# Splitting two slab loads of each looped expert by partitions, in a two-layer trunk with a mixture of experts

## Chip, cores and metric

One NeuronCore of one Trainium2 chip runs the whole kernel. The metric is the device time of one execution in microseconds (us); lower is better. The inputs lie in HBM before the start, and the output has to be in HBM at the end.

## What is computed

256 tokens of width 1024 pass two layers. Each layer has a mixer (three kinds of attention side by side) and a feed-forward part. The feed-forward part of layer 0 is dense; that of layer 1 is a mixture of eight experts, of which each token uses two. The change touches only the loads of the experts' weights.

```python
def swiglu(h, w_gate_up, w_down):
    gt, up = jnp.split(h @ w_gate_up, 2, axis=-1)
    return (jax.nn.silu(gt) * up) @ w_down

def moe_swiglu(h, w_router, w_gate_up, w_down):
    ...
    top_val, top_idx = lax.top_k(logits, TOP_K)
    top_w = jax.nn.softmax(top_val, axis=-1)
    ...
    for e in range(N_EXPERTS):
        y = y + combine[:, e:e + 1] * swiglu(t, w_gate_up[e], w_down[e])
    return y.reshape(b_, s_len, dm)
```

All of it is float32. One expert has 1024 x 7168 weights for gate and up and 3584 x 1024 for down: 42 MB in all (11.0 million numbers of four bytes).

## The kernel before

The first part (mixers, dense feed-forward part, router) ends near 735 us of the span. Its weights come in slabs of 512 KB and are of no concern here.

**Slabs of an expert.** The weights of each expert are laid out in HBM as 42 slabs (`EXP_SLABS`) of 1 MB, each 128 partitions x 2048 floats, so a partition's row of a slab is 8 KB. They are stored three by three: for each partition, the rows of three slabs (`LOAD = 3`) lie behind one another. SBUF holds a ring of 21 slabs (`exp_raw`, `EXP_RAW = 21`); slab j of any expert goes to place j % 21.

**Order of the loads.** All loads are issued by the SP engine, in the order in which TensorE reads the slabs. The first expert and the second one are loaded slab by slab (`first_slabs`, `single_slabs`, lines 583 to 607). From the third expert on a loop of the machine runs, `sp.Fori(2, slots)` at line 650, whose body is `expert_slabs` (line 609): slabs 0 to 38 in 13 loads of three slabs (3 MB, line 612), then slabs 39, 40 and 41 (`END = 39`) each as a load of its own (1 MB, line 618). Before each load SP waits on `slab_used`, a count that TensorE raises by one after the last matmul on a slab (lines 2348 and 2382); a load waits until its place in the ring is free. With these inputs eight slots are computed, one for each expert, so the loop body runs six times.

**Order of the reading.** On TensorE, `expert` (line 2328) goes through the slabs: 8 of gate and up, 8 of gate and up, 4 of down, 8 of gate and up, 4 of down, 4 of gate and up, and 6 of down. The last pieces are `down(STEPS - 2, ...)` on slabs 36 and 37, the turning of the next tokens and of the hidden values, and `down` on slabs 38, 39, 40 and 41 (lines 2412 to 2418). `wait_slab` (line 369) makes TensorE wait before a slab: on `first_ready` in the first two experts, then once per load of three on `more_ready`, and on `end_ready` for slabs 39 to 41. A load raises its semaphore by 16 when it has landed. Experts with up to 64 tokens are computed in two blocks of 32 tokens, larger ones in three (`BLOCKS_AT = (3, 2, 3, 2, 3, 3, 2)`, and two for the eighth), and TensorE needs half as long again for a slab in three blocks.

The semaphores of a loop's iteration i are waited for against a multiple of i. The first two experts don't use `more_ready` and `end_ready`, so SP raises these once by what two iterations would have given (lines 642 to 644).

```python
elif j >= END:
    pe.wait_ge(end_ready[j - END], i * 16 + 16)
...
for j in range(END, EXP_SLABS):
    sp.wait_ge(slab_used, i * EXP_SLABS + (PRE + j + 1 - EXP_RAW))
    sp.dma_start(exp_slots[j % EXP_RAW], moe_slabs[bass.ds(e, 1), j // LOAD, :, j % LOAD, :]
                 .rearrange("e p n -> (e p) n"))\
        .then_inc(end_ready[j - END], 16)
```

Of the kernel before, what the change touches and what calls it, by code (L numbers as in the profile page):

```python
# [13 lines left out]
P = 128  # L14
# [26 lines left out]
EXP_RAW, LOAD = 21, 3  # L41
SINGLE_SLOTS = 2
# [12 lines left out]
EXP_SLABS = sum(GU) + sum(DN)  # L55
# [110 lines left out]
def trunk(nc, x_in, mem_in, mix_norm_g, w_in, sb_q_g, sb_k_g, gla_a_up, gla_a_b, gla_o_g, ca_q_g,  # L166
# [10 lines left out]
    with ExitStack() as ctx:  # L177
        def sb(name, shape, dt=F32):
            return ctx.enter_context(nc.sbuf_tensor(name, shape, dt))

        def sem(name):
            return ctx.enter_context(nc.semaphore(name))
# [51 lines left out]
        exp_raw = sb("exp_raw", [P, EXP_RAW, EXP_SLAB])  # L234
# [12 lines left out]
        exp_slots = [exp_raw[:, n, :] for n in range(EXP_RAW)]  # L247
# [111 lines left out]
        end_ready = [sem(f"end_ready{i}") for i in range(LOAD)]  # L359

        END = EXP_SLABS - LOAD

        def load_ready(i, j):

            if j % EXP_RAW == END % EXP_RAW:
                return i * 16
            return i * (16 * EXP_SLABS // EXP_RAW) + 16 * (j // EXP_RAW)

        def wait_slab(pe, i, j):

            if type(i) is int and i * EXP_SLABS + j < SINGLE:
                pe.wait_ge(first_ready[j % EXP_RAW], 16 * ((i * EXP_SLABS + j) // EXP_RAW + 1))
            elif j >= END:
                pe.wait_ge(end_ready[j - END], i * 16 + 16)
            elif j % LOAD == 0:
                pe.wait_ge(more_ready[j % EXP_RAW // LOAD], load_ready(i, j))

# [32 lines left out]
        def raw_slot(j):  # L410
            return w_raw[:, j % RAW, :]
# [152 lines left out]
        @block.sync  # L564
        def _(sp):
            sp.dma_start(hn[:, 0, :], memory_in[:, 0, :]).then_inc(first_tile[0], 16)
            sp.dma_start(gain[:, :], mem_norm_g[0].rearrange("(o d) -> o d", o=1)
                         .broadcast_to([P, DM])).then_inc(first_gain, 16)
            sp.dma_start(hn[:, 1, :], memory_in[:, 1, :]).then_inc(first_tile[1], 16)
            EARLY = {20: 1, 16: 1, 15: 1, 13: 1, 12: 1, 10: 1, 4: 1, 3: 1, 2: 1, 1: 2}  # L570

            branch1 = [p for p in table if p.name == "branch1"][-1]
            last_gate = [p for p in table if p.name == "gate1"][-1]

            def first_slabs():
                for j in (0, 1, 2, 3, 4, 20, 5, 6, 7, 17, 18, 9, 10, 11, 12, 13, 14, 15, 8, 16, 19):
                    if j == 0:
                        sp.wait_ge(branch_lo, BRANCHES + 1)
                    elif j == 1:
                        sp.wait_ge(branch_lo, BRANCHES + 2)  # L580
                    elif j == 4:
                        sp.wait_ge(ca_max, LAYERS)
                    elif j == 20:
                        sp.wait_ge(slab_used, branch1.end)
                    elif j == 5:
                        sp.wait_ge(branch_lo, BRANCHES + 3)
                    elif j == 17:
                        sp.wait_ge(slab_used, last_gate.end)
                    elif j == 9:
                        sp.wait_ge(lo_ready, PRE)  # L590
                    elif j == 11:
                        sp.wait_ge(slab_used, PRE)
                    elif j == 8:
                        sp.wait_ge(norm_done, NT * 3 * LAYERS)
                    elif j == 19:
                        sp.wait_ge(route_logit, NT)
                    sp.dma_start(exp_slots[j], moe_slabs[0, j // LOAD, :, j % LOAD, :])\
                        .then_inc(first_ready[j], 16)
                    yield

            def single_slabs(e, i, js):
                for j in js:
# [3 lines that stand above are left out]
                        .then_inc(first_ready[j % EXP_RAW], 16)  # L606

            def expert_slabs(e, i, begin=0):
                for j in range(begin, END, LOAD):
                    sp.wait_ge(slab_used, i * EXP_SLABS + (PRE + j + LOAD - EXP_RAW))  # L610
                    n = j % EXP_RAW
                    sp.dma_start(exp_raw[:, n:n + LOAD, :].rearrange("p a n -> p (a n)"),
                                 moe_slabs[bass.ds(e, 1), j // LOAD]
                                 .rearrange("e p a n -> (e p) (a n)"))\
                        .then_inc(more_ready[n // LOAD], 16)
                for j in range(END, EXP_SLABS):
                    sp.wait_ge(slab_used, i * EXP_SLABS + (PRE + j + 1 - EXP_RAW))
                    sp.dma_start(exp_slots[j % EXP_RAW], moe_slabs[bass.ds(e, 1), j // LOAD, :, j % LOAD, :]
                                 .rearrange("e p n -> (e p) n"))\
                        .then_inc(end_ready[j - END], 16)  # L620

            first = first_slabs()
            for s, src in enumerate(flat):
                if s == 2:
                    sp.dma_start(xs[:, :, :], tokens).then_inc(x_loaded, 16)
                if s == 8 * RAW:
                    sp.dma_start(route_w[:, :, :], moe_router[0].rearrange("(k p) n -> p k n", p=P))\
                        .then_inc(route_loaded, 16)
                if s >= RAW:
                    sp.wait_ge(lo_ready, s - RAW + 1)  # L630
                dst = raw_slot(s)[:, 0:sizes[s]]
                if len(src.shape) == 3:
                    dst = dst.rearrange("p (k n) -> p k n", k=src.shape[1])
                sp.dma_start(dst, src).then_inc(raw_ready[s % RAW], 16)

                for _ in range(EARLY.get(PRE - s, 0)):
                    next(first)

            for _ in first:
                pass  # L640
            for n in range(EXP_RAW // LOAD):
                sp.sem_inc(more_ready[n], load_ready(SINGLE_SLOTS, n * LOAD) - 16)
            for n in range(LOAD):
                sp.sem_inc(end_ready[n], SINGLE_SLOTS * 16)
            single_slabs(0, 0, range(EXP_RAW, EXP_SLABS))
            sp.wait_ge(r_table, 1)
            slots = sp.value_load(slot_i[0:1, 0:1], min_val=EXPERTS, max_val=SLOTS)
            e = sp.value_load(slot_i[0:1, 2:3], min_val=0, max_val=EXPERTS - 1)
            single_slabs(e, 1, range(EXP_SLABS))
            with sp.Fori(2, slots) as i:  # L650
                e = sp.value_load(slot_i[0:1, bass.ds(i + 1, 1)], min_val=0, max_val=EXPERTS - 1)
                expert_slabs(e, i)
            for t in range(NT):
                sp.wait_ge(added, slots * NT + (t + 1))
                sp.dma_start(result[:, t, :], xs[:, t, :]).then_inc(stored, 16)
            sp.wait_ge(stored, NT * 16)
# [1192 lines left out]
        def _(pe):  # L1849
# [478 lines left out]
            def expert(i, blocks, blocks_ago):  # L2328
                j = 0

                def gate_and_up(s, part):
                    nonlocal j
                    w = 2 * lanes_wide(s)
                    n = KT // GU[s]
                    for q in part:
                        wait_slab(pe, i, j)
                        for kk in range(n):
                            k = q * n + kk
                            if is_first(i) and (s, k) == (0, KT // 2):
                                pe.wait_ge(x_dve, 1)  # L2340
                            for b in range(blocks):
                                for g in range(LANES):
                                    c = kk * LANES * w + g * w
                                    ins = mm(lane(pa, g)[:, b * BW:b * BW + w],
                                             xf[:, k, b * LANE:(b + 1) * LANE],
                                             exp_slots[j % EXP_RAW][:, c:c + w],
                                             k == 0, k == KT - 1)
                        ins.then_inc(slab_used, 1)
                        j += 1
# [142 lines left out]
```

## Time and profile before

| | |
|---|---|
| median of 3 runs | 1571.69 us (1571.23 to 1571.84) |
| the profiled execution's own time | 1571.44 us |
| its span, first to last instruction | 1569.6 us |
| mean granted clock of TensorE | 0.991 |
| TensorE busy with matmuls | 1534.0 us (98%) |
| VectorE, ScalarE, GpSimd busy | 521.6, 457.0, 90.3 us |
| moved by DMA | 485.63 MB, 309 GB/s on average |

The span is that of the profiled execution, and all times of the trace count from its start. PE is TensorE's matmuls, PEld its weight loads, DVE is VectorE, ACT ScalarE, POOL GpSimd, SP the engine that issues the loads. A matmul's end is modelled, so a busy TensorE isn't necessarily at its peak. The DMA share is the mean over the core's 16 DMA engines: 1.00 is all of them busy.

### The profile page before, as it was taken

The page shows a single profiled execution, that of the slowest core. Times are in us where ns is not written, and L with a number is a line of the kernel's source. Part 1 is how long each engine was busy: PE and PEld are TensorE (multiplying, and loading weights), DVE is VectorE, ACT ScalarE, POOL GpSimd, SP SyncE. Part 2 cuts the span into 40 slices and gives each one's busy share as a digit, 9 for nine tenths or more (in the row PEclk, how much of TensorE's full clock was granted, in tenths as well). Part 3 has the DMA queues.
Part 4 walks back from the last instruction along what each step waited for, and adds up shares of the span by engine and source line. Part 5 has one row for each costly group of instructions (what it writes and reads, how often), then busy time and mean ns, then how long its engine had stood idle before and what let it go on. Part 6 is the DMA issues. An engine that isn't in the chain of part 4 may idle for free.

```text
span 1569.6 us, 31360 instructions
## 1 busy us (share of the span) xinstructions
PE 1534.0 (98%) x14130; PEld 967.9 (62%) x14130; DVE 521.6 (33%) x619; ACT 457.0 (29%) x598; POOL 90.3 (6%) x128
## 2 busy tenths in 40 slices
PE   7999999999999999999999999999999999999877
PEld 6888888788888888888345453454534534544324
DVE  5755575655567565665200101001000000010001
ACT  5557653544455567452000000000000000000000
POOL 5211100000002110001000000000000000000000
PEclk9999999999999999999999999999999999999989
DMA  7555455666656554777999999999999999999995
GB/s 272 178 158 161 148 174 161 210 193 188 188 174 188 163 175 145 242 279 287 420 418 392 411 427 427 423 431 424 425 429 429 425 426 427 422 417 427 428 426 238
DMA packets 87778, 485.63 MB, mean 309 GB/s; under 512 B 10528, under 2 KB 12640, under 8 KB 64608
## 3 DMA queue, kind: packets, MB, share of 16 engines
q1 hardware_dynamic: 84592, 474.67, 78.6%
q0 software_dynamic: 3056, 8.99, 1.6%
q8 instruction: 111, 1.82, 0.5%
q14 instruction: 19, 0.16, 0.0%
HBM read 481.53 MB, written 2.10 MB: 308 GB/s over the span
## 4 chain that ended last, share of the span: by engine, by line
PE 86%; DMA 9%; DVE 2%; POOL 2%; issue 1%; ACT 0%; SPq 0%; DVEq 0%; POOLq 0%; ACTq 0%
PE pa L2075 28%; PE ps L2075 18%; PE pa L1946 12%; PE pa L1948 12%; PE pa L1947 12%; DMA exp_raw<-in_moe_slabs 8%; PE ps L2354 1%; DVE w_lo L1268 1%; DMA w_raw<-in_w_mem_kv 1%; POOL hrs L763 1%; POOL head_gains L692 0%; PE ps L2324 0%; PE ps L1873 0%; PE ps L2248 0%; PE ps L2069 0%
## 5 line engine op out<-in xcount | busy, mean ns | idle before, releaser
L2075 PE MATMUL pa<-exp_raw,xf 128*32 128x512 f32 (+1 forms) x5120 | 501.0, 544 | 14.5 <-DMA exp_raw<-in_moe_slabs 13.7
L2075 PEld LDWEIGHTS pa<-exp_raw,xf 128*32 128x32 f32 x5120 | 163.3, 110 | 308.8 <-issue 261.2
L1268 DVE TENSOR_TENSOR w_lo<-w_raw,w_hi 128x1024 fp32r<-128x1024 f32 x226 | 274.2, 1232 | 122.2 <-ACT w_hi L898 113.2
L898 ACT ACTIVATE w_hi<-w_raw 128x1024 fp32r<-128x1024 f32 (+1 forms) x228 | 236.9, 1053 | 148.9 <-PE pa L1948 146.9
L2075 PE MATMUL ps<-exp_raw,hf 128*32 128x256 f32 x4480 | 251.5, 383 | 5.5 <-DMA exp_raw<-in_moe_slabs 5.5
L1946 PE MATMUL pa<-w_hi,r 128*128 128x512 f32 x600 | 240.3, 400 | 1.9 <-DVE r L1303 1.8
L1947 PE MATMUL pa<-w_lo,r 128*128 128x512 f32 x600 | 234.6, 391 | 0.0
L1948 PE MATMUL pa<-w_hi,r 128*128 128x512 f32 x600 | 234.5, 391 | 0.0
L2075 PEld LDWEIGHTS ps<-exp_raw,hf 128*32 128x32 f32 x4480 | 146.4, 111 | 111.7 <-issue 17.6
L1821 DVE TENSOR_TENSOR hs<-pa,hs 128x768 f32<-128x768 f32 (+3 forms) x32 | 23.7, 742 | 464.9 <-ACT hs L1224 464.9
L1946 PEld LDWEIGHTS pa<-w_hi,r 128*128 128x128 f32 x600 | 113.0, 188 | 29.4 <-issue 3.2
L1948 PEld LDWEIGHTS pa<-w_hi,r 128*128 128x128 f32 x600 | 113.0, 188 | 24.2
L1947 PEld LDWEIGHTS pa<-w_lo,r 128*128 128x128 f32 x600 | 113.2, 189 | 22.0
L1946 PE MATMUL pa<-w_hi,xt 128*128 128x512 f32 (+1 forms) x320 | 123.2, 385 | 3.0 <-DVE xt L1303 2.7
L1948 PE MATMUL pa<-w_hi,xt 128*128 128x512 f32 (+1 forms) x320 | 121.3, 379 | 0.0
L1947 PE MATMUL pa<-w_lo,xt 128*128 128x512 f32 (+1 forms) x320 | 121.2, 379 | 0.0
L1224 ACT ACTIVATE hs<-pa 128x768 f32<-128x768 f32 (+3 forms) x32 | 20.4, 637 | 314.7 <-PE pa L2075 314.7
L1214 ACT ACTIVATE hf<-ps 128x512 f32<-128x512 f32 x24 | 14.3, 597 | 290.5 <-PE ps L2354 290.5
L1946 PEld LDWEIGHTS pa<-w_hi,xt 128*128 128x128 f32 x320 | 60.2, 188 | 16.1 <-issue 2.7
L1948 PEld LDWEIGHTS pa<-w_hi,xt 128*128 128x128 f32 x320 | 60.2, 188 | 11.3
L1947 PEld LDWEIGHTS pa<-w_lo,xt 128*128 128x128 f32 x320 | 60.3, 188 | 10.6
L1808 DVE COPY hf<-ps 128x256 f32<-128x256 f32 x12 | 5.1, 424 | 163.4 <-PE ps L2354 163.4
(274 smaller groups left out, 859.3 us busy)
## 6 DMA issues: line engine op xcount, KB each, us to landing
exp_raw<-in_moe_slabs SPq DMA_DIRECT2D x78, 3072.0 KB, 31.3
exp_raw<-in_moe_slabs SPq DMA_DIRECT2D x102, 1024.0 KB, 10.2
w_raw<-in_w_in SPq DMA_DIRECT2D x104, 512.0 KB, 4.4
w_raw<-in_ff_w_gate_up SPq DMA_DIRECT2D x44, 512.0 KB, 4.5
w_raw<-in_ff_w_down SPq DMA_DIRECT2D x22, 512.0 KB, 4.1
w_raw<-in_w_mem_kv SPq DMA_DIRECT2D x16, 512.0 KB, 5.5
w_raw<-in_w_out SPq DMA_DIRECT2D x16, 512.0 KB, 4.3
w_raw<-in_w_br_sb SPq DMA_DIRECT2D x8, 512.0 KB, 3.6
```

The costliest lines, as they stand in the source:

```text
L763: pool.tensor_tensor(dst[:, 0:n], src[:, 0:n], half[:, 0:n], ALU.pow)\
L898: act.activation(dst, raw, ACT.Copy).then_inc(hi_ready, 1)
L1214: act.activation(hf[:, s % 2, 0:m, :], turned_hidden(s)[:, 0:m, :], ACT.Copy)\
L1224: act.activation(hidden_rows(s, blocks), gate_up(s, 0, blocks), ACT.Silu)\
L1268: dve.tensor_tensor(dst, raw, hi.bitcast(F32), ALU.subtract)\
L1808: dve.tensor_copy(hf[:, s % 2, 4:2 * blocks, :], turned_hidden(s)[:, 4:2 * blocks, :]).then_inc(e_dve, 1)
L1821: dve.tensor_tensor(hidden_rows(s, blocks), gate_up(s, 1, blocks), hidden_rows(s, blocks), ALU.mult).then_inc(e_h, 1)
L1946: pe.matmul(dst, hi, m_hi, start=first, stop=False)
L1947: pe.matmul(dst, hi, m_lo, start=False, stop=False)
L1948: return pe.matmul(dst, lo, m_hi, start=False, stop=last)
L2075: return pe.matmul(dst, a, b, start=start, stop=stop, skip_group_check=True)
L2354: ins = pe.transpose(turned_hidden(s)[:, m, :], hs[:, m * P:(m + 1) * P], ident[:, :])
```

## The change

Each of slabs 39 and 40 of a looped expert is loaded by three DMAs in place of one: partitions 0 to 111, partitions 112 to 119, and partitions 120 to 127, all with 8 KB per partition as before. Slab 41, the loads of three slabs, and the first two experts stay as they are. By its description the load of 112 partitions is done by all 16 DMA engines (seven rows each) and each load of eight partitions by the low eight of them (one row each). Every part raises the slab's `end_ready` semaphore by 16, so the multiple that TensorE waits for is 48 in place of 16 for slabs 39 and 40, and SP's one-time raise is three times as large for these.

```diff
         END = EXP_SLABS - LOAD
+        LOW_DMAS = P // 16
+        PARTS = [(0, P - 2 * LOW_DMAS), (P - 2 * LOW_DMAS, P - LOW_DMAS), (P - LOW_DMAS, P)]
+
+        def end_parts(j):
+
+            return PARTS if j < EXP_SLABS - 1 else [(0, P)]
...
             elif j >= END:
-                pe.wait_ge(end_ready[j - END], i * 16 + 16)
+                n = 16 * len(end_parts(j))
+                pe.wait_ge(end_ready[j - END], i * n + n)
...
                 for j in range(END, EXP_SLABS):
                     sp.wait_ge(slab_used, i * EXP_SLABS + (PRE + j + 1 - EXP_RAW))
-                    sp.dma_start(exp_slots[j % EXP_RAW], moe_slabs[bass.ds(e, 1), j // LOAD, :, j % LOAD, :]
-                                 .rearrange("e p n -> (e p) n"))\
-                        .then_inc(end_ready[j - END], 16)
+                    for a, b in end_parts(j):
+                        sp.dma_start(exp_raw[a:b, j % EXP_RAW, :],
+                                     moe_slabs[bass.ds(e, 1), j // LOAD, a:b, j % LOAD, :]
+                                     .rearrange("e p n -> (e p) n"))\
+                            .then_inc(end_ready[j - END], 16)
...
             for n in range(LOAD):
-                sp.sem_inc(end_ready[n], SINGLE_SLOTS * 16)
+                sp.sem_inc(end_ready[n], SINGLE_SLOTS * 16 * len(end_parts(END + n)))
```

On the other engines the order of the instructions is the same. On SP, these are the rows at the end of the loop's body before (the last load of three slabs, then slabs 39, 40 and 41; `exp_raw` is the ring, `in_moe_slabs` the weights in HBM):

```order
L612 DMA exp_raw<-in_moe_slabs 128x6144
L617 REGISTER_ALU
L618 ISA [waits slab_used]
L618 DMA exp_raw<-in_moe_slabs 128x2048
L617 REGISTER_ALU
L618 ISA [waits slab_used]
L618 DMA exp_raw<-in_moe_slabs 128x2048
L617 REGISTER_ALU
L618 ISA [waits slab_used]
L618 DMA exp_raw<-in_moe_slabs 128x2048
L650 REGISTER_ALU
```

And these stand there on SP now, from slab 40 to the loop's end (slab 39 is as slab 40):

```order
L624 REGISTER_ALU
L626 ISA [waits slab_used]
L626 DMA exp_raw<-in_moe_slabs 112x2048
L626 ISA
L626 DMA exp_raw<-in_moe_slabs 8x2048
L626 ISA
L626 DMA exp_raw<-in_moe_slabs 8x2048
L624 REGISTER_ALU
L626 ISA [waits slab_used]
L626 DMA exp_raw<-in_moe_slabs 128x2048
L659 REGISTER_ALU
```

One wait still stands ahead of each slab. Two DMAs of eight partitions follow that of 112 without a wait, and slab 41's load stands behind them: four DMAs more in each pass of the loop.

## Rows read from the trace of the kernel before

**Rows 1.** The page: busy tenths, granted clock and DMA in 40 slices of the span.

```profile
PE   7999999999999999999999999999999999999877
PEclk9999999999999999999999999999999999999989
DMA  7555455666656554777999999999999999999995
GB/s 272 178 158 161 148 174 161 210 193 188 188 174 188 163 175 145 242 279 287 420 418 392 411 427 427 423 431 424 425 429 429 425 426 427 422 417 427 428 426 238
```

**Rows 2.** Waits of PE, 745 to 1450 us: who, for whom, us, times, longest.

```profile
PE pa L2075 <- DMA exp_raw<-in_moe_slabs: 2.8, 1, 2.8
PE pa L2075 <- DVE hs L1821: 0.8, 1, 0.8
PE ps L2075 <- DMA exp_raw<-in_moe_slabs: 0.4, 1, 0.4
```

**Rows 3.** The same view, 1450 to 1562 us.

```profile
PE pa L2075 <- DMA exp_raw<-in_moe_slabs: 10.9, 8, 2.0
PE ps L2075 <- DMA exp_raw<-in_moe_slabs: 5.1, 3, 3.6
```

**Rows 4.** Chain that ended last, from 1440 us: start us, us, what.

```profile
1453.14 43.30 DMA exp_raw<-in_moe_slabs
...
1502.06 47.69 DMA exp_raw<-in_moe_slabs
1549.75 0.14 issue
1549.88 3.66 PE ps L2075 x64
1553.55 1.02 PE ps L2324 x8
1554.57 0.22 PE pa L2354 x2
1554.79 7.09 PE ps L2075 x128
```

**Rows 5.** Timeline of PE, last expert: start, us, instructions, [idle before <- releaser].

```profile
1520.54 5.36 PE L2075 MATMUL pa<-exp_raw,xf 128*32 128x512 f32 x48 [1.17 <-DMA exp_raw<-in_moe_slabs]
1527.84 3.28 PE L2075 MATMUL pa<-exp_raw,xf 128*32 128x512 f32 x16 [1.95 <-DMA exp_raw<-in_moe_slabs]
...
1535.17 3.66 PE L2075 MATMUL ps<-exp_raw,hf 128*32 128x256 f32 x64 [0.26 <-DMA exp_raw<-in_moe_slabs]
...
1542.50 1.93 PE L2075 MATMUL pa<-exp_raw,xf 128*32 128x256 f32 x32 [1.94 <-DMA exp_raw<-in_moe_slabs]
...
1549.88 3.66 PE L2075 MATMUL ps<-exp_raw,hf 128*32 128x256 f32 x64 [1.27 <-DMA exp_raw<-in_moe_slabs]
```

**Rows 6.** Windows: stretch, length, busy by engine, clock, DMA share, GB/s.

```profile
1540.00:1544.00 4.00, 2.06 (x40) 1.02 (x36) 0.00 (x0) 0.00 (x0) 0.00 (x0) 1.00 1.02 426
1545.00:1547.00 2.00, 2.00 (x41) 1.23 (x44) 0.00 (x0) 0.60 (x1) 0.00 (x0) 1.00 0.51 217
1547.00:1550.00 3.00, 1.73 (x36) 0.85 (x32) 0.42 (x1) 0.38 (x1) 0.00 (x0) 1.00 0.46 191
1550.00:1553.00 3.00, 3.00 (x60) 2.18 (x61) 0.00 (x0) 0.00 (x0) 0.00 (x0) 1.00 0.51 213
1553.00:1556.00 3.00, 3.00 (x46) 1.94 (x42) 0.42 (x1) 0.66 (x2) 0.00 (x0) 1.00 0.43 169
1556.00:1558.00 2.00, 2.00 (x45) 1.19 (x39) 0.00 (x0) 0.00 (x0) 0.00 (x0) 1.00 0.07 25
```

**Rows 7.** DMA by queue, 745 to 1558 us: packets, MB, share of 16 engines.

```profile
q1 hardware_dynamic: 23422, 334.10, 97.4%
q0 software_dynamic: 1315, 4.80, 1.5%
q8 instruction: 82, 1.34, 0.7%
q14 instruction: 5, 0.04, 0.0%
```

**Rows 8.** Source view of L612, loads of three slabs: ns min/median/max; us to landing.

```profile
L612 SPq DMA_DIRECT2D exp_raw<-in_moe_slabs x78: 332/333/337, 907.0 to 1502.1; - x78
...
DMA to landing us min/median/max: 19.7/31.3/48.4
```

**Rows 9.** Source view of L618, slabs 39 to 41: ns min/median/max; us to landing.

```profile
L618 SPq FUSED_REGOPS  x18: 37/37/37, 994.8 to 1513.7; - x18
L618 SPq MOVE exp_raw<-in_moe_slabs x18: 29/29/29, 994.9 to 1513.8; - x18
L618 SPq DMA_DIRECT2D exp_raw<-in_moe_slabs x18: 332/333/333, 994.9 to 1513.8; - x18
...
DMA to landing us min/median/max: 25.3/32.9/43.4
```

## The prediction, made before the changed kernel ran

> **What bounds the kernel now.** I read the page's slices first. From slice 20 on (about 745 us) the DMA row stands at 9 and the rate at 392 to 431 GB/s, up to the last slice [rows 1]. TensorE stands at 9 there as well, so two resources look full, and the waits have to tell which one sets the end. From 745 to 1450 us TensorE waits 3.2 us in all for slabs [rows 2], from 1450 us on 16.0 us, in eleven waits (8 + 3) [rows 3]. TensorE is behind while experts come in three blocks, and catches up in the last ones. The chain that ended last says the same: two long pieces of DMA lead to 1549.75 us, then TensorE works without a stop to about 1561.9 us [rows 4]. The wait that ends at 1549.88 us is for the load that holds slabs 36 to 38 of the last expert. So the end is that landing plus a fixed tail of matmuls, scatter and store, and the landing is the end of an unbroken stream of transfers. **A microsecond off the stream ahead of that landing is a microsecond off the end**, until the 16.0 us of waits are used up.
>
> Is the stream ever dry? A load of three slabs never lands in less than 19.7 us after its issue, and the single slabs take 25.3 us or more [rows 8, 9]. The waits of the last expert end at 1520.54, 1527.84, 1535.17, 1542.50 and 1549.88 us, about 7.33 us apart [rows 5], so three slabs need 7.33 us. At least 12 us of work is always queued. SP's issuing sets nothing.
>
> Now the look that matters for this change: are the 16 DMA engines equally late? The windows over the end say no. The DMA share is 1.02 up to 1544 us, then 0.51, 0.46, 0.51 and 0.43 from 1545 to 1556 us, then 0.07 [rows 6]. **Half of the engines finish their part of the stream near 1545 us, the other half near 1556 us, some 10.5 us later**, and TensorE waits for the late half each time. Each engine has the same rows of weights to move, so the late ones do something else besides. The queues show it: 82 instruction packets of 16 KB (1.34 MB), 0.7% of 16 engines' time in 813 us, which is 0.007 x 16 x 813 = 91 us of engine time, about 1.1 us each [rows 7]. Spread over eight engines that is 11.4 us each, close to the 10.5 us; over all 16 there would be no two halves. I take it that TensorE's instructions are fetched by eight of the engines.
>
> **The change, part by part.** *Rows moved.* A slab is eight rows of 8 KB for each engine. Slabs 39 and 40 become seven rows for each engine and two more for the low eight: nine for these, seven for the high eight. A row costs 7.33 / 24 = 0.305 us (24 rows of a load of three, on the late half) [rows 5]. The landing that sets the end is that of slabs 36 to 38 of the sixth pass; ahead of it lie five passes with two split slabs each, ten slabs. If the late half is the high half, its stream is ten rows shorter: 10 x 0.305 = **3.05 us earlier**. The early half gets 3.05 us more and still finishes 10.5 - 6.1 = 4.4 us ahead. Slabs 39 and 40 of the sixth pass are moved behind the deciding wait: the stream ends before 1558 us with slab 41 [rows 6], so slab 40 is there a slab's time earlier, before 1556 us; slabs 38 to 41 are read in turn in 7.09 us from 1554.79 us on [rows 4], slab 40 from 1558.3 us. They are in time and stay so. Worth 0 there.
>
> *More DMAs on SP.* Four more in each pass, each 37 + 29 + 333 ns [rows 9]: 1.6 us. Ahead of every landing lie at least 12 us of queued work [rows 5, 8], so this is hidden: 0. If that cover were gone, it would be 1.6 us per pass, 8 us by the deciding wait.
>
> *More completion marks.* Three where there was one. The trace doesn't show what one costs an engine; single slabs and loads of three have one mark for 8 and for 24 rows. As a bound, the whole difference between the share of the loads, 97.4%, and full use, less instructions and the small queue, is 100 - 97.4 - 1.5 - 0.7 = 0.4% of 813 us, 3.3 us for the marks of all 159 loads, 0.02 us each [rows 7]. The low engines get two more in each of ten slabs, the high ones none: at most 0.4 us, on the early half. 0 on the path.
>
> *Where the rows land.* In a load of 128 partitions every engine writes partitions that are its own. A load of eight partitions has eight engines writing at once to eight neighbouring partitions, and the 112 are dealt out in other portions. No transfer of this size on fewer than 128 partitions is in the trace, so nothing prices it. The lower bound is no cost, since it's the same number of rows of 8 KB; a gain over 0.305 us a row has no reason, as the engines are full. The upper bound is that the engines of such a load are served in turn. I take no cost, the nearest row being the ordinary row time, and keep the turns for a rival. The break-even: the low half has 4.4 us in hand after the move, so its split slab may cost 0.44 us more than nine plain rows before it becomes the late half, and 10.5 - 3.05 = 7.45 us, so 0.75 us a slab, before the kernel is slower than now.
>
> **Sum** against the profiled execution: 1571.44 - 3.05 = 1568.39 us. Its own time is 0.25 us under the median of the runs, 1571.69 us; against that, 1571.69 - 3.05 = **1568.6 us**. A measurement of this kernel can tell about 0.2% from no change, which is 3.14 us. So my forecast lies on that edge, and I split its chance evenly.
>
> **Rivals.**
>
> *Served in turn (slower).* Suppose four of the eight engines of a small load share one way into SBUF. Then its row takes 4 x 0.305 = 1.22 us in place of 0.305, twice per slab: 1.83 us more. The low half loses 10 x (0.305 + 1.83) = 21.4 us by the deciding landing, has 10.5 us in hand, and ends 10.9 us later than the late half does now: 1571.69 + 10.9 = **1582.6 us**. If the high engines, whose rows go to the same partitions, are held up too (half of the 1.22 us a slab), another 6 us: 1588. For it: the rate of 425 GB/s over so long [rows 1] says that whatever is full has no room to catch up. Against it: writes could be buffered, and the early half can spare 7.45 us. It decides from 0.75 us a slab. The Trainium skill speaks for this rival (SBUF — State Buffer, section Door 1: the DMA port swizzle): the 128 partitions hang on 16 ports, four neighbours to a port, so partitions 112 to 119 reach only two ports, and its measured table gives four partitions 27.6 GB/s against 328 for all. Eight rows of 8 KB through two such ports would take, as an estimate from that page, 1.2 us, and the time would be this rival's. No run here shows it yet.
>
> *Partly eaten.* A smaller cost of the same kind, 0.45 to 0.75 us a slab: the low half becomes the late one and the gain shrinks from 3.05 to 0 us. 1568.7 to **1571.7**.
>
> *The late half is not the high half.* No view names a DMA engine, so the trace can't say which eight fetch instructions. If they are the low ones (or some of them are), the change loads the late engines with ten rows more: 1571.69 + 3.05 = **1574.7 us**. Nothing in the rows speaks for or against; it could as well be half, and 0.12 is a judgement.
>
> *It doesn't do what it says.* If the loads of eight partitions were dealt to all or to high engines, the late half would gain less than ten rows or lose some; that lies between 1568.6 and 1574.7, in the cases above.
>
> **How the numbers follow.** The forecast, 1568.6 (own range 1567.8 to 1569.3), has 0.50. A gain a little above the edge for reasons I don't see: 0.02, faster. Partly eaten: 0.10, no change. Low half is the late one: 0.12, at +3.05 us just under the edge, so half no change and half slower. Served in turn: 0.26, slower. Faster by over 0.2%: 0.25 + 0.02 = 0.27. Within: 0.25 + 0.10 + 0.06 = 0.41. Slower: 0.06 + 0.26 = 0.32. For eight times in ten the range takes in all but the last rival (0.74) and the near quarter of that one: from 1567.3 to 1580.0 us.
>
> **What would show it.** Right: the stretch of half DMA share before the end shrinks from 10.5 to about 4.4 us less a slab's share; the wait that ended at 1549.88 us ends near 1546.8; TensorE's waits from 1450 us on sum to about 13.0 us in place of 16.0. Served in turn: DMA share stays near 1 while GB/s falls in the stretch where slabs 39 and 40 are served, once per pass, and the half-share stretch at the end is gone or turned round. Low half late: the half-share stretch grows from 10.5 to some 16.6 us, with the last wait near 1553. Wrong altogether: the last wait at 1549.9 with an unchanged stretch, or waits of TensorE for slab 39 or 40 in the middle passes.

## The result, and the profile after

Each kernel ran four times. The changed one took 1649.89 us (median; 1646.38 to 1653.89), the one before 1571.76 us (1571.23 to 1572.61). The ratio is 1.0494 (95% interval 1.0482 to 1.0507): **slower by 78.1 us, 13.0 us for each of the six passes of the loop**. The forecast was 1568.6 us, and the range ended at 1580.0 us. The profiled execution of the changed kernel took 1646.38 us by its own time, 74.9 us more than that of the kernel before.

The page of the changed kernel, busy tenths and DMA in 40 slices of its span (41.1 us each):

```profile
PE   8999999999999999999999999996899999976776
PEclk9999999999999999999999999999999999998998
DMA  7555444766565555779999999999999999999994
GB/s 270 176 161 165 142 154 157 242 186 194 160 203 179 164 154 186 277 287 417 414 386 415 427 426 364 385 427 319 425 427 295 429 425 265 428 427 273 429 405 144
```

The row to read is the last one, against [rows 1]. The DMA row stays at 9 as before, but the rate, which held 392 to 431 GB/s from slice 20 on, now falls to 364 and 385, 319, 295, 265 and 273 GB/s, once in each of the first five passes. The engines are as busy as ever and move less. The windows over two of these places show how deep the holes are (columns as in [rows 6]; the DMA share and the rate stand last):

```profile
1000.00:1010.00 10.00, 10.00 (x98) 3.31 (x94) 0.39 (x1) 0.39 (x1) 0.00 (x0) 1.00 1.00 427
1010.00:1020.00 10.00, 10.00 (x100) 3.08 (x96) 0.03 (x1) 0.20 (x1) 0.00 (x0) 1.00 1.02 348
1020.00:1030.00 10.00, 10.00 (x192) 6.25 (x186) 0.96 (x1) 0.81 (x1) 0.00 (x0) 1.00 1.00 194
1030.00:1040.00 10.00, 8.41 (x144) 6.37 (x140) 0.42 (x1) 0.60 (x1) 0.00 (x0) 1.00 1.04 314
1040.00:1050.00 10.00, 10.00 (x177) 6.25 (x167) 0.64 (x2) 0.57 (x2) 0.00 (x0) 1.00 0.99 419
...
1360.00:1390.00 30.00, 27.99 (x442) 14.55 (x438) 1.38 (x2) 1.41 (x2) 0.00 (x0) 1.00 1.02 224
...
1605.00:1610.00 5.00, 3.11 (x60) 1.60 (x52) 0.00 (x0) 0.00 (x0) 0.00 (x0) 1.00 1.00 224
1610.00:1616.00 6.00, 0.00 (x0) 0.00 (x0) 0.00 (x0) 0.00 (x0) 0.00 (x0) 0.65 0.87 202
1616.00:1619.00 3.00, 2.89 (x28) 1.38 (x32) 0.00 (x0) 0.00 (x0) 0.00 (x0) 0.50 0.81 254
1619.00:1622.00 3.00, 3.00 (x24) 1.31 (x20) 0.00 (x0) 0.60 (x1) 0.00 (x0) 0.50 0.50 186
```

At a DMA share of 1.00 the rate is 194 GB/s from 1020 to 1030 us; in the kernel before the same stretch reads thus:

```profile
1020.00:1030.00 10.00, 10.00 (x192) 6.05 (x188) 0.79 (x1) 0.00 (x0) 0.00 (x0) 1.00 1.04 437
```

The hole at 1360 us lasts 30 us at 224 GB/s. At 427 GB/s the same bytes take 30 x 224 / 427 = 15.7 us, so this pass lost 14.3 us there. The holes aren't all alike: the same sum over windows of 10 us between 1010 and 1616 us gives about 10, 11, 13, 15, 15 and 8 us for the six passes, 72 us in all, beside the 74.9 us between the two profiled executions. **30 us at 224 GB/s are 6.7 MB, but only two slabs, 2.1 MB, were split**: the whole loads that are served beside them are held up too.

What TensorE waited for, from 745 to 1450 us (as [rows 2]):

```profile
PE pa L2084 <- DMA exp_raw<-in_moe_slabs: 11.2, 4, 6.4
PE ps L2084 <- DMA exp_raw<-in_moe_slabs: 9.7, 2, 7.7
PE pa L2084 <- issue: 4.8, 3, 2.0
PE ps L2084 <- issue: 3.5, 2, 2.0
```

And from 1450 us on (as [rows 3]):

```profile
PE pa L2084 <- DMA exp_raw<-in_moe_slabs: 32.7, 12, 8.0
PE ps L2084 <- DMA exp_raw<-in_moe_slabs: 16.1, 7, 4.7
```

The waits grew by 29.2 - 3.2 = 26.0 us in the first stretch and by 48.8 - 16.0 = 32.8 us in the second. (Of the 29.2 us, 8.3 us are put down to "issue", idle time for which the profile shows no releaser; that they are waits for loads isn't shown.) The other 16.9 us are matmuls that take longer: TensorE is busy for 1550.9 us in place of 1534.0 us. The granted clock over the whole execution is 0.979 in place of 0.991; after an idle stretch such as 1610 to 1616 us it stands at 0.50, which is 1.2 GHz. 26.0 + 32.8 + 16.9 = 75.7 us, against the 74.9 us to be explained. TensorE computes nothing more; it waits, and then runs slower for a while.

The timeline of PE in the last expert (as [rows 5]) shows which landing now sets the end:

```profile
1601.04 5.35 PE L2084 MATMUL ps<-exp_raw,hf 128*32 128x256 f32 x64 [2.77 <-DMA exp_raw<-in_moe_slabs]
...
1616.11 3.64 PE L2084 MATMUL pa<-exp_raw,xf 128*32 128x256 f32 x32 [8.00 <-DMA exp_raw<-in_moe_slabs]
...
1624.83 3.63 PE L2084 MATMUL ps<-exp_raw,hf 128*32 128x256 f32 x64
```

Before, the last wait was for slabs 36 to 38 and ended at 1549.88 us. Now it is for the load ahead of that one (before: 1542.50 us), lasts 8.00 us, and there is none after it. That load is in flight together with the split slabs of the same pass. So the sixth pass costs time as well, and twelve slabs count, not ten.

### The profile page after: what moved, and what is told of

It is laid out like the page before. It is cut to its first block, busy times and chain, and to the rows that moved or that the text cites. A ratio compares the mean times of both kernels' runs of the same rounds, so it can differ in the third digit from the quotient of the medians.

```text
span 1644.6 us, 31433 instructions
## 1 busy us (share of the span) xinstructions
PE 1550.9 (94%) x14130; PEld 974.2 (59%) x14130; DVE 521.5 (32%) x619; ACT 457.2 (28%) x598; POOL 90.3 (5%) x128
## 4 chain that ended last, share of the span: by engine, by line
PE 83%; DMA 9%; another core or an unknown queue 2%; DVE 2%; POOL 2%; issue 1%; ACT 0%; SPq 0%; DVEq 0%; POOLq 0%; ACTq 0%
PE pa L2084 27%; PE ps L2084 18%; PE pa L1955 12%; PE pa L1957 11%; PE pa L1956 11%; DMA exp_raw<-in_moe_slabs 8%; PE ps L2363 1%; DMA w_raw<-in_w_mem_kv 1%; DVE w_lo L1277 1%; POOL hrs L772 1%; PE ps L2333 0%; POOL head_gains L701 0%; PE ps L1882 0%; PE ps L2257 0%
## 5 line engine op out<-in xcount | busy, mean ns | idle before, releaser
L2084 PE MATMUL pa<-exp_raw,xf 128*32 128x512 f32 (+1 forms) x5120 | 507.6, 547 | 49.6 <-DMA exp_raw<-in_moe_slabs 43.9
L2084 PE MATMUL ps<-exp_raw,hf 128*32 128x256 f32 x4480 | 260.3, 389 | 29.3 <-DMA exp_raw<-in_moe_slabs 25.8
L1223 ACT ACTIVATE hf<-ps 128x512 f32<-128x512 f32 x24 | 14.3, 598 | 324.2 <-PE ps L2363 324.2
```

The source lines that it names most:

```text
L1223: act.activation(hf[:, s % 2, 0:m, :], turned_hidden(s)[:, 0:m, :], ACT.Copy)\
L2084: return pe.matmul(dst, a, b, start=start, stop=stop, skip_group_check=True)
```

## The experiments

I held two theories at first, and a third that both had to beat. **P**: the load of 112 partitions costs the time, because its rows fall to other DMA engines than those of a whole load do. **Q**: the loads of eight partitions cost it, four engines on one way into SBUF, as in my rival. **R**: the number of DMAs or marks costs it. Two more came later: **W**, P and Q in one, that in a whole load each engine has a way into SBUF of its own, and that an engine which writes on another's way slows both; and **S**, that anything under 128 partitions is slow. In e1, e2, e3, e7 and e8 the rest of slabs 39 and 40 of a looped expert isn't loaded, so their times are of fewer bytes. All diffs are against the changed kernel.

### e1 and e2: each kind of load alone

```diff
-        PARTS = [(0, P - 2 * LOW_DMAS), (P - 2 * LOW_DMAS, P - LOW_DMAS), (P - LOW_DMAS, P)]
+        PARTS = [(0, P - 2 * LOW_DMAS)]
```

> This one leaves out the loads of partitions 112 to 127 of slabs 39 and 40 of the looped experts: only the load of 112 partitions stays. Theory P (the 112 are the cost: each engine's seven rows fall on ways into SBUF that other engines use, so all of them slow down while such a load is served): nearly all of the 78 us stay, above 1630 us. Theory Q (the loads of eight are the cost, four engines in turn on one way): the stream is one row per engine and slab shorter, ten slabs by the deciding wait, 1571.7 - 3.05 = about 1568.7 us. Theory R (the number of DMAs and completion marks is the cost): 1568.7 us too.

```diff
-        PARTS = [(0, P - 2 * LOW_DMAS), (P - 2 * LOW_DMAS, P - LOW_DMAS), (P - LOW_DMAS, P)]
+        PARTS = [(P - 2 * LOW_DMAS, P - LOW_DMAS), (P - LOW_DMAS, P)]
```

> Leaves out partitions 0 to 111 of slabs 39 and 40: only the two loads of eight partitions stay. Plain rows would make the late half's stream eight rows per slab shorter, 24 us by the deciding wait, of which TensorE's 16.0 us of waits can be gained: about 1555 to 1557 us. P: that. Q: the two small loads keep most of the 6.5 us per split slab, so 1571.7 + 78 - 24, above 1610 us. R: two DMAs in place of three, a gain less than under P but below 1571.7 us.

Measured: e1 1634.7 us and e2 1572.61 us, the kernel before beside them 1572.29 us, one run of each. The load of 112 partitions, with nothing beside it, brings 62.4 of the 78 us, though it moves an eighth less. That is what P foresaw; Q and R are too small by over 60 us. The window of e1 over the first hole:

```profile
1020.00:1030.00 10.00, 9.69 (x178) 5.60 (x174) 0.96 (x1) 0.81 (x1) 0.00 (x0) 1.00 1.02 212
```

e2 is not as harmless as its time looks, since it moves only an eighth of the two slabs. It met none of the three expectations: P had 1555 to 1557 us, Q above 1610 us, R a gain. Its rate in the same place is 357 GB/s at full share:

```profile
1020.00:1030.00 10.00, 10.00 (x192) 6.03 (x188) 0.96 (x1) 0.81 (x1) 0.00 (x0) 1.00 1.00 357
```

### e3, e7 and e8: the loads of eight, on other partitions

Three variants of e2 differ only in which partitions the sixteen rows of each split slab go to: four apart in the upper half (e3), four apart in the lower one (e7), side by side in the lower one (e8). The lines of e3, e7 and e8 in that order; the loads take a stride in the first two.

```diff
-        PARTS = [(0, P - 2 * LOW_DMAS), (P - 2 * LOW_DMAS, P - LOW_DMAS), (P - LOW_DMAS, P)]
+        PARTS = [(64, 96, 4), (65, 97, 4)]
...
+        PARTS = [(0, 32, 4), (1, 33, 4)]
...
+        PARTS = [(0, LOW_DMAS), (LOW_DMAS, 2 * LOW_DMAS)]
```

> As e2_only_eights, but the eight partitions of each load are four apart (64, 68, ... 92 and 65, 69, ... 93) in place of neighbours, the same bytes and the same number of engines and DMAs. Leaves out the other 112 partitions. Q: neighbours share a way and partitions four apart don't, so this one is back at about 1555 to 1557 us while e2 isn't. P and R: the same time as e2_only_eights.

> As e3_spread_eights (the other 112 partitions of slabs 39 and 40 left out), but the eight partitions lie in the low half, four apart: 0, 4, ... 28 and 1, 5, ... 29. Theory W (16 ways into SBUF, a way for partitions four apart and for the same group 32 further on; a full load gives each DMA engine a way of its own, the low engines those of partitions 0 to 63): now no engine writes another's way, and the time falls to what TensorE's waits allow, about 1555 to 1557 us. Theory S (any load of fewer than 128 partitions is slow, wherever it lands): 1568 us, as e3_spread_eights.

> As e2_only_eights, but with the neighbours 0 to 7 and 8 to 15, in the low half. W: the eight low engines crowd on two ways of their own half, so only the early half is held up, each row four row times, and the high half isn't touched: early half 5 passes x 4 rows x 0.9 us = 18 us minus 30 rows saved (9 us), inside its lead of 10.5 us, so the time is again about 1555 to 1558 us. S: 1572 us, as e2_only_eights.

| kernel | partitions | us | before | difference |
|---|---|---|---|---|
| e2 | 112 to 119, 120 to 127 | 1572.61 | 1572.29 | +0.3 |
| e3 | 64, 68 ... 92; 65, 69 ... 93 | 1568.10 | 1572.29 | -4.2 |
| e8 | 0 to 7; 8 to 15 | 1565.55 | 1571.28 | -5.7 |
| e7 | 0, 4 ... 28; 1, 5 ... 29 | 1553.01 | 1571.28 | -18.3 |

Same bytes, same number and size of loads, same engines by the description: the choice of partitions alone is worth 18.6 us. The windows from 1015 to 1035 us, one line each of e3, e7 and e8:

```profile
1015.00:1035.00 20.00, 20.00 (x332) 10.65 (x328) 0.96 (x1) 0.81 (x1) 0.00 (x0) 1.00 1.01 367
```

```profile
1015.00:1035.00 20.00, 20.00 (x336) 11.08 (x332) 1.32 (x2) 1.17 (x2) 0.00 (x0) 1.00 1.02 431
```

```profile
1015.00:1035.00 20.00, 20.00 (x332) 10.79 (x325) 0.96 (x1) 0.81 (x1) 0.00 (x0) 1.00 1.00 365
```

Only e7 keeps the full rate. S falls with it: loads of eight partitions aren't slow as such. Its size fits a plain sum too. An engine that carries two rows of a split slab in place of eight saves 6 x 0.305 us, 18.3 us over the ten slabs ahead of the landing that decides, and 18.3 us were measured. Part of this fit can be luck: the page of e7 has 409, 372 and 395 GB/s in its slices from 1280 to 1396 us, so its stream wasn't full all the time. Measured against e7, the crowding cost about 18.3 + 0.3 = 18.6 us in e2, 14.1 us in e3 and 12.6 us in e8. e3 and e8 both missed: e3 lies between Q's 1555 to 1557 us and e2's time, and e8 is 7.5 us above what W gave. e3 and e8 have one run each, and the seven runs of the kernel before beside e7 and e8 spread from 1570.38 to 1574.13 us, so the 1.5 us between their costs say nothing; writing side by side in the low half costs about what writing four apart in the high half costs.

### e4 and e5: other contiguous parts, the whole slab loaded

```diff
-        PARTS = [(0, P - 2 * LOW_DMAS), (P - 2 * LOW_DMAS, P - LOW_DMAS), (P - LOW_DMAS, P)]
+        PARTS = [(0, P - 2 * LOW_DMAS), (P - 2 * LOW_DMAS, P)]
```

> All work done, slabs 39 and 40 in two loads: partitions 0 to 111, and 112 to 127 as one load of sixteen, one row for each of 16 engines. P: about as slow as the change, 1640 to 1650 us. Q: the sixteen rows go by four ways with four engines each, once per slab and not twice, so about half of the cost: 1600 to 1615 us. R: two thirds of the marks, about 1620 us.

```diff
-        PARTS = [(0, P - 2 * LOW_DMAS), (P - 2 * LOW_DMAS, P - LOW_DMAS), (P - LOW_DMAS, P)]
+        PARTS = [(0, P // 2), (P // 2, P)]
```

> All work done, slabs 39 and 40 each in two loads of 64 partitions, four rows for each of 16 engines. If several engines on one way is what costs (the mechanism under P and Q), each half of the partitions has half of the ways, two engines on each: half the rate for two slabs, 2.46 us more per slab by itself, 12 slabs, so at least 1571.7 + 25 = 1597 us. R: two DMAs in place of three, less than 1630 us and more than 1572 us. If only uneven dealing of 112 costs: 1571.7 us, no change.

Measured: e4 1640.42 us (before 1572.29), e5 1640.77 us (before 1572.55), +68.1 and +68.2 us. Two parts of 64 partitions cost nearly as much as the change does. The window of e5:

```profile
1020.00:1030.00 10.00, 9.62 (x178) 5.59 (x174) 0.96 (x1) 0.00 (x0) 0.00 (x0) 1.00 0.98 210
```

The 112 is nothing special, then, and neither are portions of seven rows. e4 came out as P said. e5 is on the side that I had given to several engines on one way, but its size isn't explained by that alone: two slabs at half the rate are 2 x 2.46 = 4.9 us a pass, 29.5 us in six, and 68.2 us were lost. The other 39 us lie in the whole loads beside them.

### e6: three loads of each slab, by columns

```diff
-        PARTS = [(0, P - 2 * LOW_DMAS), (P - 2 * LOW_DMAS, P - LOW_DMAS), (P - LOW_DMAS, P)]
+        PARTS = [(0, 1024), (1024, 1536), (1536, EXP_SLAB)]
...
-                        sp.dma_start(exp_raw[a:b, j % EXP_RAW, :],
-                                     moe_slabs[bass.ds(e, 1), j // LOAD, a:b, j % LOAD, :]
+                        sp.dma_start(exp_raw[:, j % EXP_RAW, a:b],
+                                     moe_slabs[bass.ds(e, 1), j // LOAD, :, j % LOAD, a:b]
```

> All work done, slabs 39 and 40 each in three loads of all 128 partitions by columns (1024, 512 and 512 floats): the same number of DMAs, completion marks and semaphore steps as the change, but every engine writes its own partitions. R: as slow as the change, 1640 to 1650 us. P and Q: 1571.7 us within 2 us (rows of 4 KB and 2 KB in place of 8 KB for 4 percent of the slabs).

Measured: 1572.46 us, before 1572.55 us. The same number of DMAs on SP, the same marks and waits, rows of 2 and 4 KB, and no cost; 434 GB/s where e5 has 210:

```profile
1020.00:1030.00 10.00, 10.00 (x193) 5.98 (x184) 0.68 (x1) 0.00 (x0) 0.00 (x0) 1.00 1.06 434
```

R is out, and my two zeros for SP's issues and for the marks stand.

### e13: halves by odd and even partitions

```diff
-        PARTS = [(0, P - 2 * LOW_DMAS), (P - 2 * LOW_DMAS, P - LOW_DMAS), (P - LOW_DMAS, P)]
+        PARTS = [(0, P, 2), (1, P, 2)]
```

> All work done, slabs 39 and 40 each in two loads of 64 partitions: the even ones and the odd ones. Dealt in order, four to an engine, each engine's rows stay in its own half of the partitions but on two ways, one of them shared with one other engine of its half. Theory W, shared ways cost and crossing into the other half is the worst of it, as the other half is then held up in its whole loads: less than e5_two_64 (1640.8 us), by half the rate for two slabs about 1590 to 1600 us. If any sharing costs alike: about 1640 us. Theory S (whatever is not 128 partitions is slow) is out by e7.

The loads take the stride, as in e3. Measured: 1571.32 us, before 1572.33 us, one run each. That misses what I expected, 1590 to 1600 us: nothing is lost at all. It speaks against W as I had worded it, since by that wording each engine shares a way with another one here. With e5 it is the cleanest pair of the study: e5 and e13 load the same slabs in two parts of 64 partitions and the same bytes, and are 69 us apart.

```profile
1020.00:1030.00 10.00, 10.00 (x192) 6.05 (x188) 0.61 (x1) 0.00 (x0) 0.00 (x0) 1.00 1.03 430
```

**In this pair, parts that reach over the whole range of partitions keep the rate, and parts that are one contiguous half of it halve the rate.** The Trainium skill (SBUF — State Buffer, Door 1: the DMA port swizzle) says that partitions 0 to 63 reach only eight of 16 ports, for some 218 GB/s in the limit; the 210 GB/s of e5 agree, though more bytes than the two split slabs went at that rate. By the table of that section every other partition reaches all 16 ports, and e13's 430 GB/s agree.

### e9 and e12: more rows for the low engines, without another way in

To test the other premise, that the late half is the high half, both kernels load slabs whole, as before, and add small DMAs of eight rows from HBM to HBM, whose results nobody reads: two for each of slabs 39 and 40 in e9, four in e12.

```diff
-        PARTS = [(0, P - 2 * LOW_DMAS), (P - 2 * LOW_DMAS, P - LOW_DMAS), (P - LOW_DMAS, P)]
+        PARTS = [(0, P)]
...
+                    if j < EXP_SLABS - 1:
+                        for b in range(2):
+                            sp.dma_start(spare[j - END, b],
+                                         moe_slabs[bass.ds(e, 1), j // LOAD, b:b + 32:4, j % LOAD, :]
+                                         .rearrange("e p n -> (e p) n"))\
+                                .then_inc(spare_ready, 16)
```

> The full computation with whole loads of all slabs, as before the change, plus four loads of eight rows of 8 KB in each pass, from HBM to a spare place in HBM: four rows more for the low engines, none for the high ones, and nothing of it enters SBUF. If the high half is the late one, the lead of 10.5 us covers 20 rows (6.1 us or somewhat more) by the deciding wait: 1572 us, no change. If the low engines are the late half: 6 us or more later, 1578 us or above.

> As e9_low_extra with twice the spare rows: eight loads of eight rows in each pass, from HBM to HBM. In e9 the end came 3.4 us later and in its last 4 us the DMA share stood at 0.12 to 0.14, two engines of 16. If two of the late eight are among the low eight, these two carry twice the load now: 7 to 8 us later than before, 1579 to 1580 us, with a longer stretch at 2/16 share at the end. If instead the spare transfers only disturbed the stream in general, all engines are later and no such stretch is seen. If the late half is the high half after all: 40 rows are 12 us, the low ones become the late ones by a little, 1573 to 1576 us, and the last stretch has a share of 8/16.

Measured: e9 1575.64 us (before 1571.28), +4.4; e12 1583.59 us (before 1572.33), +11.3. Both missed their numbers: e9 lies between its two cases, 1572 us and 1578 us or above, and e12 above the 1579 to 1580 us for two late engines among the low eight. At 0.305 us a row the deciding landing comes 20 x 0.305 = 6.1 and 40 x 0.305 = 12.2 us later on an engine that was among the late ones. TensorE's wait for it ends at 1553.93 us in e9 and at 1560.64 us in e12, 4.1 and 10.8 us later than before. On an early engine, with 10.5 us in hand, e9 would show nothing and e12 1.7 us. So some of the low eight were late already, if somewhat less than the others: 1.4 to 2.0 us less, should a row from HBM to HBM cost what any other row costs, which no run shows. How many, the windows say, first those of e9, then those of e12:

```profile
1545.00:1550.00 5.00, 3.46 (x56) 2.02 (x60) 0.00 (x0) 0.60 (x1) 0.00 (x0) 1.00 0.85 352
1550.00:1553.00 3.00, 2.65 (x52) 1.31 (x42) 0.00 (x0) 0.28 (x1) 0.00 (x0) 1.00 0.54 224
1553.00:1556.00 3.00, 2.07 (x40) 1.57 (x44) 0.42 (x1) 0.10 (x1) 0.00 (x0) 1.00 0.45 188
1558.00:1560.00 2.00, 2.00 (x32) 1.40 (x34) 0.42 (x1) 0.66 (x2) 0.00 (x0) 1.00 0.12 41
1560.00:1562.00 2.00, 2.00 (x44) 1.17 (x37) 0.00 (x0) 0.00 (x0) 0.00 (x0) 1.00 0.14 53
```

```profile
1553.00:1556.00 3.00, 2.75 (x44) 1.57 (x48) 0.00 (x0) 0.20 (x1) 0.00 (x0) 1.00 0.82 341
1557.00:1559.00 2.00, 2.00 (x44) 1.17 (x36) 0.00 (x0) 0.00 (x0) 0.00 (x0) 1.00 0.20 82
1559.00:1562.00 3.00, 1.72 (x36) 1.04 (x32) 0.42 (x1) 0.38 (x1) 0.00 (x0) 1.00 0.12 52
1562.00:1565.00 3.00, 3.00 (x51) 2.12 (x44) 0.00 (x0) 0.00 (x0) 0.00 (x0) 1.00 0.13 52
1565.00:1568.00 3.00, 3.00 (x53) 1.89 (x55) 0.42 (x1) 0.66 (x2) 0.00 (x0) 1.00 0.12 46
1568.00:1571.00 3.00, 2.86 (x56) 1.43 (x45) 0.00 (x0) 0.00 (x0) 0.00 (x0) 1.00 0.11 41
```

In e9 the share falls in steps, 0.85, about 0.5 and about 0.13: 14, eight and two engines of 16. In e12 fourteen engines are done by 1559 us, and a share of 0.11 to 0.13 for another 11 us is two engines of 16. Ahead of the very end lie all six passes, 48 extra rows in e12 or 14.6 us. By the arithmetic, six low engines that were early end near 1545 + 14.6 = 1559.6 us, six high ones where they did, near 1556 us, and two low ones, late before and loaded with the extra rows as well, near 1570.6 us. (In e12 TensorE waits for slab 41 too, until 1572.03 us.) No view names an engine; this is a count by shares. **The late half is six of the high engines and two of the low ones.** e7 is in line with it: its 18.3 us are the six rows that a low engine sheds; the high ones shed eight, 24.4 us.

### e10: the same shift of rows, with no load of 112

Slab 39 is loaded as 128 partitions x 1536 floats, and its last 512 floats by sixteen loads of eight partitions that lie four apart, on the low engines by the description; slabs 40 and 41 are whole. In bytes this moves as much to the low engines as the change does.

```diff
-        PARTS = [(0, P - 2 * LOW_DMAS), (P - 2 * LOW_DMAS, P - LOW_DMAS), (P - LOW_DMAS, P)]
+        WIDE = 3 * EXP_SLAB // 4
...
+                    if j == END:
+                        sp.dma_start(exp_raw[:, j % EXP_RAW, 0:WIDE],
...
+                        for a in range(0, P, 32):
+                            for b in range(a, a + 4):
+                                sp.dma_start(exp_raw[b:min(b + 32, P):4, j % EXP_RAW, WIDE:EXP_SLAB],
```

> The shift that the change aims at, without crowding: slab 39 as one load of 128 partitions by 1536 floats and, for the last 512 floats, sixteen loads of eight partitions four apart. The low engines move two rows' worth more in each pass and the high ones two less, as in the change. If DMA engines are what is full, 3 us faster: 1568.6 us. W: half of the sixteen use the ways of the high engines, which are as full as these engines, so nothing is gained and the sharing costs: 1572 to 1577 us. Seventeen issues on SP (7.5 us a pass) stay behind at least 12 us of queued work: 0.

Measured, with four runs: 1586.81 us (1585.19 to 1588.50), before 1571.28 us, ratio 1.0101 (1.0084 to 1.0118): 15.5 us slower, and a miss. The tidy shift gains nothing either.

```profile
1015.00:1035.00 20.00, 20.00 (x332) 10.82 (x325) 0.96 (x1) 0.81 (x1) 0.00 (x0) 1.00 1.01 395
```

Two low late engines with ten rows more explain 3.05 us. The other 12.5 us go with the rate of 395 GB/s; half of the small loads write to the upper 64 partitions, where e3 lost its time too. That this half is the reason was not tried, nor were seventeen loads for one slab priced by themselves (e6 has three).

## Why the prediction was wrong

**What failed first: "Where the rows land".** The prediction had said that nothing in the trace prices a transfer of this size on fewer than 128 partitions, and then took no cost. Its words on the 112 were "dealt out in other portions", and all bounds were worked out for the loads of eight. Measured: the load of 112 brings 62.4 us in e1, with one row of a split slab fewer on each engine (ten rows, 3.05 us), so its price is about 65.5 us, an estimate: **5.5 us for each of twelve slabs, where the term was 0 and the break-even 0.75 us**. Adding the loads of eight brings 15.2 us more (1649.89 - 1634.7), of which 20 rows on two low late engines are 6.1 us and some 9 us crowding, good to a few us only, as e1 ran once and the runs of the changed kernel lie 7.5 us apart. The sixth pass, "worth 0 there", lost some 8 us ahead of the last wait.

**Served in turn** was the rival with the right kind of cause: a share near 1 with a falling rate, once per pass, as its test said, and the half-share stretch at the end shrunk. It was priced for the loads of eight alone, 10.9 us, with 6 us for the engines held up by them, 1588 at most. Most of the time is not in the rows of the split slabs, but in the 4.6 MB of whole loads that went at half rate beside them.

**What failed second: the late half is the high half.** It is six high engines and two low ones. At the plain price of a row, with no crowding at all, the change would have made these two the last by ten rows: up to 1574.7 us, the figure of the rival that had 0.12. The gain of 3.05 us was never there.

**What held.** The stream of transfers sets the end, and TensorE shows it as waits: with fewer rows e7 took 1553.01 us, and its last wait for a load ended at 1531.43 us in place of 1549.88 us. A row at 0.305 us on the late engines fits e7 (18.3 us worked out by it, 18.3 us measured, with some luck) and less well e9 (6.1 and 4.1 us). SP's four more DMAs and the marks cost nothing (e6). Eight of 16 engines end 10.5 us late (e12's windows are in line with it). But the share I gave the slower side, 0.32, came from two premises that no row showed; between bounds of 0 and an unknown, "the nearest row" was no evidence for 0.

**What stays open.** How a load of 112 is dealt to the engines can't be seen in a view; that whole loads keep the rate because each engine has a way of its own is a reading of e5 and e7, not shown engine by engine, and e13 lost nothing though engines would share ways there if rows are dealt out in order, which no view shows. By the Trainium skill (DMA: Bandwidth & Descriptors, The descriptor swizzle) a whole load gives each engine the partitions of one port, the low eight engines partitions 0 to 63. That sets e7 (own ports, no loss) apart from e8 (own half, four engines on a port), e3 (one engine on each port of the high engines) and e2 (four on a port of the high half, the largest loss), as they came out; no run here reads the ports. Why the whole loads beside a contiguous part are held up so long is open as well. One rival was left untested: the partitions of a load also choose the rows that it reads in HBM, 24 KB apart. e3 and e7 read with the same stride, 1.5 MB apart, and differ by 14.1 us, which speaks for the writing side without settling it. Whether the loss grows evenly with the number of split slabs was not tried. No version that loads everything beat the kernel before: e6 and e13 equal it, with one run each.

## What to carry to other kernels

Where a stream of loads is the bound, a load's set of partitions is part of its price: here a split by columns (e6) or into odd and even partitions (e13) was free, every split of a whole slab into contiguous ranges (the change, e4, e5) cost 68 to 78 us, and the bad pieces slowed the good loads around them. Read GB/s beside the DMA share in every window, since a share of 1.00 stood for 437 and for 194 GB/s here. And before moving work off the late engines, find out which they are, with a small extra load as in e9.

## What the runs showed of the hardware that I had not expected

- Two loads of 64 partitions cost 68.2 us over twelve slabs when the halves are contiguous (1640.77 us), and nothing when they are the even and the odd partitions (1571.32 us).
- In one pass 2.1 MB of split slabs held the whole stream at 224 GB/s for 30 us, 6.7 MB.
- Sixteen rows of 8 KB per slab, 24 loads in all, differ by up to 18.6 us in what they cost by their partitions alone (e7, e8, e3, e2).
- The eight engines that end late at the end of the stream are not one of the two halves: by the shares of e9 and e12, two of them are among the low eight.
